# Down projection by seven block products in a fused two-block transformer kernel

## The reference, cut to what matters

```python
h2 = rms_norm_2(x, g_ffn)                                  # x: 512 x 1024
act = silu(h2 @ w_ffn_gate) * (h2 @ w_ffn_up)              # 512 x 2816
x = x + act @ w_ffn_down                                   # 2816 x 1024
return rms_norm_2(x, g_final)
```

## Time and profile before

| | us |
|---|---|
| median of 3 runs (1060.65 to 1061.04) | 1060.84 |
| the profiled execution, its span (the profile gives no other time of it) | 1059.3 |
| TensorE busy | 1049.7 (99%) |
| VectorE, ScalarE, GpSimd busy | 509.0 (48%), 448.8 (42%), 400.2 (38%) |
| HBM read and written | 92.80 MB and 2.12 MB |

### The profile page before, as it was taken

The page is one execution under the profiler, slowest core; times in us unless marked ns, Lnnn a source line. Parts: engine busy times, 40 slices in busy tenths (PEclk is TensorE's granted clock), DMA queues, the critical chain, the costliest instruction groups (busy, mean ns, idle before and its releaser), DMA issues.

```text
span 1059.3 us, 14455 instructions
## 1 busy us (share of the span) xinstructions
PE 1049.7 (99%) x5545; PEld 844.1 (80%) x5545; DVE 509.0 (48%) x1061; ACT 448.8 (42%) x788; POOL 400.2 (38%) x300
## 2 busy tenths in 40 slices
PE   9999999999999999999999999999999999999997
PEld 8877897767678876888777888888888888888886
DVE  6766788875752316998587344230000000032444
ACT  6444457676653425233465414342221221233533
POOL 3455520001025333446000255434435354465772
PEclk9999999999999999999999999999999999999999
DMA  9541141201032331332221232223232323323221
GB/s 298 184 120 51 34 119 41 75 17 44 28 120 80 72 117 43 101 99 80 80 80 41 80 104 95 91 77 110 80 118 79 114 84 104 114 80 100 82 97 80
DMA packets 84724, 95.72 MB, mean 90 GB/s; under 512 B 8121, under 2 KB 70930, under 8 KB 84666
## 3 DMA queue, kind: packets, MB, share of 16 engines
q1 hardware_dynamic: 83706, 92.46, 28.0%
q0 software_dynamic: 560, 2.12, 0.6%
q10 hardware_dynamic: 400, 0.35, 0.1%
HBM read 92.80 MB, written 2.12 MB: 90 GB/s over the span
## 4 chain that ended last, share of the span: by engine, by line
PE 94%; DVE 4%; ACT 1%; issue 1%; POOL 0%; DVEq 0%; ACTq 0%; POOLq 0%
PE bank L1882 56%; PE bank L2194 23%; PE bank L1940 4%; PE bank L1971 3%; PE bank L2012 3%; PE bank L1988 1%; DVE L L1478 1%; PE bank L2169 1%; PE bank L1833 1%; PE bank L2098 1%; PE bank L2045 1%; DVE L L1524 1%; DVE pool L1483 0%; PE bank L2001 0%; PE bank L1964 0%
## 5 line engine op out<-in xcount | busy, mean ns | idle before, releaser
L1042 POOL TENSOR_TENSOR w_lo<-raw,w_hi 128x512 fp32r<-128x512 f32 (+1 forms) x190 | 267.2, 1436 | 415.7 <-ACT w_hi L1104 403.0
L1882 PE MATMUL bank<-h_hi,w_hi 128*128 128x512 f32 (+1 forms) x560 | 224.0, 400 | 0.3 <-ACT h_hi L1315 0.2
L1882 PE MATMUL bank<-h_hi,w_lo 128*128 128x512 f32 (+1 forms) x560 | 218.6, 390 | 0.0
L1882 PE MATMUL bank<-h_lo,w_hi 128*128 128x512 f32 (+1 forms) x560 | 217.8, 390 | 0.0
L1082 POOL TENSOR_TENSOR w_lo<-raw,w_hi 128x512 fp32r<-128x512 f32 x88 | 110.7, 1290 | 133.5 <-ACT w_hi L1353 67.1
L1104 ACT ACTIVATE w_hi<-raw 128x512 fp32r<-128x512 f32 (+3 forms) x94 | 111.2, 1213 | 116.1 <-PE bank L1882 113.8
L1882 PE MATMUL bank<-w_hi,h_hi 128*128 128x512 f32 (+2 forms) x397 | 145.3, 366 | 0.0
L1882 PE MATMUL bank<-w_lo,h_hi 128*128 128x512 f32 (+2 forms) x397 | 144.5, 364 | 0.0
L1882 PE MATMUL bank<-w_hi,h_lo 128*128 128x512 f32 (+2 forms) x397 | 144.5, 364 | 0.0
L2194 PE MATMUL bank<-h_hi,w_hi 128*128 128x512 f32 x352 | 137.1, 389 | 0.0
L2194 PE MATMUL bank<-h_hi,w_lo 128*128 128x512 f32 x352 | 137.0, 389 | 0.0
(11 more groups left out here) (213 smaller groups left out, 1260.3 us busy)
## 6 DMA issues: line engine op xcount, KB each, us to landing
raw<-in_w_in SPq DMA_DIRECT2D x29, 1024.0 KB, 5.3
raw<-in_w_ffn_gate SPq DMA_DIRECT2D x11, 1024.0 KB, 5.4
raw<-in_w_ffn_up SPq DMA_DIRECT2D x11, 1024.0 KB, 5.4
raw<-in_w_out SPq DMA_DIRECT2D x8, 1024.0 KB, 5.0
raw<-in_w_ffn_down SPq DMA_DIRECT2D x8, 1024.0 KB, 5.1
raw<-in_w_in SPq DMA_DIRECT2D x8, 512.0 KB, 4.6
pool<-in_cmp_w SPq DMA_DIRECT2D x4, 1024.0 KB, 9.1
raw<-in_w_ffn_down SPq DMA_DIRECT2D x4, 768.0 KB, 4.3
```

The costliest lines, as they stand in the source:

```text
L1042: nc.gpsimd.tensor_tensor(w_lo[:, u.n % 2, cols], raw[:, u.n % 2, cols], w_hi[:, u.n % 2, cols].bitcast(F32), ALU.subtract).then_inc(lo_do ...
L1882: ins = mm(bank[t.bank][0:t.m, 0:u.width if u.token else T], stationary, moving, start=first and n == 0, stop=last and n == len(products) ...
```

## The change

With A the activations (rows: tokens, 0 to 255 and 256 to 511; columns: even and odd feature tiles) and B the weights (rows: even and odd tiles; columns: the two halves), the eight block products of A times B are replaced by seven with sums of blocks (Winograd's form of Strassen's scheme):

- on the activations: s1 and s2, the left factors of p5 and p6 (s1 from the blocks `s1` and `a22` of the buffer, s2 from s1 and `a11`), and s3 = a22 - s2 and s4 = a12 - s2, the left factors of p7 and p3;
- on the weights: t1 to t4, four sums of 128x512 per pair of weight tiles.

Each product has 11 weight tiles in units of 4, 4 and 3, and two token tiles (256 tokens). The order is p1, p6, p7, p5, p4, p3, p2. p3 and p2 go on accumulating in the banks of p5 and p1. p1 is copied out by ScalarE (kind "lead"); p6 and p7 are added by VectorE in two instructions each ("second", "third"); p5, p4, p3 and p2 end rows ("residual"). Rows 2 and 3 are finished before rows 0 and 1.

The sums of the activations s1 and s2 and all weight sums are made by VectorE in the feed-forward steps; the weight sums are stored in HBM by SyncE and loaded back as units. The temporaries s3 and s4 are made by VectorE unit by unit during the down projection. In all units but the first the low part of the first 512 columns is GpSimd's, the rest VectorE's, and ScalarE's high part is made in two instructions.

The diff, cut to its core:

```diff
+    def product_units(name, left_, right, banks, kind, tiles, more=False):
+        tiles = [Tile(0, P, kind, idx) for idx in tiles]
+        for f, n in ((0, 4), (4, 4), (8, 3)):
+            u = Unit(name, [(right(f, n), 0, 512)], n, 512, tiles, k0=f, first=f == 0, last=f == 8, act=True, token=True)
...
+    FIRST_ROWS, LATER_ROWS = (0, 1), (2, 3)
+    down_u = (product_units("p1", "a11", lambda f, n: down_block(0, 0, f, n), (0, 1), "lead", FIRST_ROWS)
+              + product_units("p6", "s2", lambda f, n: down_sum(1, f, n), (2, 3), "second", FIRST_ROWS)
+              + product_units("p7", "s3", lambda f, n: down_sum(2, f, n), (4, 5), "third", FIRST_ROWS)
+              + product_units("p5", "s1", lambda f, n: down_sum(0, f, n), (6, 7), "residual", [(1, i) for i in LATER_ROWS])
+              + product_units("p4", "a22", lambda f, n: down_sum(3, f, n), (4, 5), "residual", [(0, i) for i in LATER_ROWS])
+              + product_units("p3", "s4", lambda f, n: down_block(1, 1, f, n), (6, 7), "residual", [(1, i) for i in FIRST_ROWS],
+                              more=True)
+              + product_units("p2", "a12", lambda f, n: down_block(1, 0, f, n), (0, 1), "residual", [(0, i) for i in FIRST_ROWS],
+                              more=True))
+    LAST_ORDER = LATER_ROWS + FIRST_ROWS
+    POOL_PART = 1
...
-    project(down_u, RING4, 4)
+    for u in down_u:
+        for j, t in enumerate(u.tiles):
...
+            if j == 0 and next_of[u.n] is not None:
+                emit("split", u=next_of[u.n], of=u)
...
+            emit("matmuls", u=u, t=t, j=j, ks=range(u.nk), end=True, part=part, fresh=None)
+            if u.last and t.kind == "residual":
+                evacuated(t)
...
         def _(sp):
             def load(u):
                 if u.n >= 2:
-                    wait_free(sp, [(order[u.n - 2].lo_by, order[u.n - 2].lo_end)])
+                    wait_free(sp, order[u.n - 2].lo_all)
...
+            def load_blocks(f):
+                sp.dma_start(zs[:, 0:2, :], wdown.rearrange("(r p) n -> p r n", p=P)[:, bass.ds(f * 2, 2), :]).then_inc(blocks_in, 16)
+            def store_sums(f):
+                sp.wait_ge(sums_made, f * 1 + 1)
+                sp.dma_start(sums_dram[:, bass.ds(f * 2048, 2048)], zs[:, 2:4, :].rearrange("p a n -> p (a n)"))\
+                  .then_inc(sums_stored, 16)
+            ffn_loads(0)
+            ffn_loads(1)
+            sp.wait_ge(tile_done, ffn_at["tile"] + 1)
+            load_blocks(0)
+            with sp.Fori(2, FFN_STEPS) as f:
+                ffn_loads(f)
+                store_sums(f - 2)
+                load_blocks(f - 1)
+            store_sums(FFN_STEPS - 2)
+            load_blocks(FFN_STEPS - 1)
             sp.dma_start(gfin, a["g_final_2"].to_broadcast([P, D])).then_inc(gfin_in, 16)
             for u in down_u:
+                if u is down_u[3]:
+                    store_sums(FFN_STEPS - 1)
+                if u.summed:
+                    sp.wait_ge(sums_stored, 16 * (u.k0 + u.nk))
                 load(u)
...
         # ScalarE, at "split"
+                    if e["u"].shared:
+                        split_hi(e["u"], slice(0, POOL_PART * PIECE))
+                        split_hi(e["u"], slice(POOL_PART * PIECE, e["u"].nk * PIECE))
+                        split_act_hi(e["u"])
...
         # VectorE, at "split"
+                if kind == "split" and e["u"].shared:
+                    ahead_ = e["u"].act0 + 1
+                    if ahead_ < len(down_u) and down_u[ahead_] in temps:
+                        make_temp(down_u[ahead_])
+                    split_shared(e["u"])
+                    split_act_lo(e["u"])
...
+            def split_shared(u):
+                ve.wait_ge(hi_done, u.hi_end)
+                cols = slice(POOL_PART * PIECE, u.nk * PIECE)
+                v.tensor_tensor(w_lo[:, u.n % 2, cols], raw[:, u.n % 2, cols], w_hi[:, u.n % 2, cols].bitcast(F32),
+                                ALU.subtract).then_inc(lo_dve, 1)
...
+                if kind == "second":
+                    chain(v.tensor_tensor(L[:, idx, :], src[:, :], L[:, idx, :], ALU.add))
+                    v.tensor_tensor(x, x, L[:, idx, :], ALU.add).then_inc(second_done, 1)
+                if kind == "third":
+                    chain(v.tensor_tensor(L[:, idx, :], src[:, :], L[:, idx, :], ALU.add))
+                    x = xres[:, 2 + idx, :].rearrange("p (c n) -> p c n", n=512)
+                    v.tensor_tensor(x, x, spread(L[:, idx, 0:1], [0, 2], [1, 512]), ALU.add).then_inc(third_done, 1)
...
+                    def left_sums(f):
+                        v.tensor_tensor(s1, s1, left_pair(f, LEFT["a22"]), ALU.add).then_inc(left_made, 1)
+                        v.tensor_tensor(left_pair(f, LEFT["s2"]), s1, left_pair(f, LEFT["a11"]), ALU.subtract)\
+                            .then_inc(left_made, 1)
+                    def block_sums(f, first=False):
+                        ve.wait_ge(blocks_in, f * 16 + 16)
...
+                        v.tensor_tensor(t1, block_in[:, 0, 1, :], block_in[:, 0, 0, :], ALU.subtract).then_inc(sum_step, 1)
+                        v.tensor_tensor(t3, block_in[:, 1, 1, :], block_in[:, 0, 1, :], ALU.subtract)
+                        v.tensor_tensor(t2, block_in[:, 1, 1, :], t1, ALU.subtract).then_inc(sum_step, 1)
+                        v.tensor_tensor(t4, block_in[:, 1, 0, :], t2, ALU.subtract).then_inc(sums_made, 1)
...
+                    gated_step(0)
+                    block_sums(0, first=True)
+                    gated_step(1)
+                    with ve.Fori(2, FFN_STEPS - 1) as f:
+                        block_sums(f - 1)
+                        gated_step(f)
+                    block_sums(FFN_STEPS - 2)
+                    gated(FFN_STEPS - 1, 0, left_pair(FFN_STEPS - 1, 0, 512))
                     split_act_lo(down_u[0])
-                    gated(FFN_STEPS - 1, 1, act[:, NFF - 1, :])
+                    gated(FFN_STEPS - 1, 1, left_pair(FFN_STEPS - 1, 512, 512))
+                    left_sums(FFN_STEPS - 1)
+                    block_sums(FFN_STEPS - 1)
```

More of the change, by code:

```diff
@@ L693, in build @@
         u.used = ("tile_done", ffn_at["tile"] + 2 * j + 2)
-    turn[RING4] = 0
-    project(down_u, RING4, 4)
-    flush()
+    ffn_end = count["tile_done"]
+    for u in down_u:
+        for j, t in enumerate(u.tiles):
+            if u.first:
+                t.bank = u.banks[j]
+                t.waits = left[t.bank]
+            if j == 0 and next_of[u.n] is not None:
+                emit("split", u=next_of[u.n], of=u)
+            unit_end = j == len(u.tiles) - 1
+            t.done = upto("tile_done") if u.last else None
+            part = upto("part_done") if unit_end and not u.last else None
+            if unit_end:
+                u.used = ("part_done", part) if part else ("tile_done", t.done)
+            emit("matmuls", u=u, t=t, j=j, ks=range(u.nk), end=True, part=part, fresh=None)
+            if u.last and t.kind == "residual":
+                evacuated(t)
+            elif u.last:
+                t.nth = upto(t.kind + "_done")
+                left[t.bank] = [(t.kind + "_done", t.nth)]
+                emit("evacuate", t=t)
     units_before_ffn = order[:ffn_u[0].n]
@@ L1011, in _, with ffn_loads @@
             n0 = ffn_u[0].n
[L1012 removed]
+            def ffn_loads(f):
                 for j, w in enumerate((wg, wu)):
@@ L1216, in row @@
                 else:
-                    if half == 0 and i == 0:
+                    if (half, i) == ((1, LAST_ORDER[0]) if nth == 3 else (0, 0)):
                         act_fn(st[:, ST_RS + NT:ST_RS + NT + 1], eps, ACT.Sqrt)
@@ L1685, in last_rows @@
             def last_rows(half, i, res):
-                if half and i == NT - 1:
+                final, p = half == 0, LAST_ORDER.index(i)
+                if final and p == NT - 1:
                     ve.wait_ge(squares, squares_at(3, half, i))
@@ L1689, in last_rows @@
                                     st[:, ST_BASE + i:ST_BASE + i + 1], ALU.mult, ALU.add).then_inc(base_done, 1)
-                if half and i == 0:
-                    ve.wait_ge(squares, squares_at(3, 0, NT - 1))
-                    v.tensor_scalar(st[:, ST_BASE:ST_BASE + NT], st[:, ST_SS:ST_SS + NT], 1.0 / D, EPS, ALU.mult, ALU.add)\
-                        .then_inc(base_done, 1)
-                if half:
-                    gained(half, i, res)
-                if half and i != NT - 2:
+                if final and p in (0, 2):
+                    ve.wait_ge(squares, squares_at(3, 1, i + 1))
+                    v.tensor_scalar(st[:, ST_BASE + i:ST_BASE + i + 2], st[:, ST_SS + i:ST_SS + i + 2], 1.0 / D, EPS,
+                                    ALU.mult, ALU.add).then_inc(base_done, 1)
+                gained(half, i, res)
+                if final and p != NT - 2:
                     last_row(i)
@@ L1881, in matmuls @@
                         wait_free(pe, [(h_hi_at, h_lo_at)[p][fresh, u.k0 + k]])
```

(4 more changed lines are left out.)

187 lines of the change are left out of this document (131 added, 56 removed).

## The result

| | before | after |
|---|---|---|
| median, us (range, runs) | 1060.86 (1060.65 to 1061.04, 4) | 1083.32 (1081.06 to 1084.01, 4) |
| span of the profiled execution, us | 1059.3 | 1081.8 |
| ratio after / before | | 1.0208, 95% interval 1.0194 to 1.0223 |

The change made the kernel 2.1% slower, 22.5 us. Forecast were +13.5 us and a range up to 1081. The direction was right, the size was not, and the measured time lies outside the range.

A forecast was written before the change was run, and what follows sets the result against it. The down projection was taken to be bound by TensorE alone. Terms -15.0 + 7.2 + 12.0 + 9.8 - 0.5 = +13.5 on 1060.8 gave 1074.3 us, range 1065 to 1081.

The forecast's parts named there:

- Removed matmuls: Down projection: seven block products instead of eight, 462 matmuls instead of 528, 15.0 us less.
- First units: Start of each product after the first: TensorE waits 1.2 us for a_lo, six times, 7.2 us.
- Second units: Second units of products: evacuations and row work delay their splits, longest wait 4.8 us after p4, sum 12.0 us.
- Hand-over: Feed-forward to down projection: late first load and VectorE's queue make the second down unit start 9.8 us late.
- Taking turns: Hand-over: VectorE and GpSimd alternate, one whole instruction each; without it and with the load in time, 1.6 us.
- The reading as both running slower: Hand-over: VectorE and GpSimd slow side by side, by 27% and 40%; second unit near 944, sum 4.4 us smaller.
- Tail: End of kernel: one row instead of three before the last tile, so its second half is evacuated earlier, -0.5 us.
- rival 3: Down projection: clock also falls in two new gaps, one or two units at double pitch, 1077 to 1084; chance 0.13.

The follow-up runs named there:

- e4: The changed kernel with the activations' high and low parts and temporaries made one unit further ahead; 1068.19 us.
- e5: The changed kernel with evacuations and row work of a product's two tiles moved behind the split of the next product's second unit; 1070.97 us.
- e2: The changed kernel with the first down unit's load issued on SyncE ahead of the store of step 9's sums; 1077.51 us.
- e9: The changed kernel with first down load issued first, last block sums behind the second unit's splits, their store before the sixth unit's load; 1072.86 us.
- e1: The changed kernel with float32 matmuls on constants queued on TensorE before five of its long waits; 1075.76 us.
- e7: The changed kernel with first down load first, last block sums late, activations one unit further ahead, row work behind the next product's second-unit split; 1058.88 us.
- e10: The changed kernel with half of the low parts on GpSimd instead of a quarter; 1088.22 us.
- e11: e8 with two float32 fill matmuls before the first unit of p2; 1053.95 us.
- e8: e7 with the last sums' store before the sixth unit's load and row work's two tiles split behind the successor's second and third units; 1056.16 us.

## Why the prediction was right and wrong

- **Removed matmuls, -15.0**: right, same pitch.
- **First units, 7.2**: right (7.6). e4 took a_lo out of the chain and the waits went.
- **Second units, 12.0**: right in sum (12.1), and that near by luck: the longest was 5.7, not 4.8, and two others 0.4 shorter than forecast. That the evacuations queue behind the next first unit's splits, and that row work holds w_hi, both read from the earlier trace rows, is borne out by e5, which moved the two together and nothing else.
- **Hand-over, 9.8**: right (9.0). The load landed at 931.8 (932.7 forecast), the last block sum of step 9 ended at 919.7 (919.6), a_lo of u1 at 947.9 (948.5). e2 and e9 show that both the load and VectorE's queue are behind it; the load moved alone did not suffice (e2), the sums moved alone were not run.
- **Taking turns**: right; 5.57 for four a_lo (1.54 in e2 without GpSimd) and 2.29 for the one of u1 are waits for GpSimd pieces. The reading as both running slower, with 4.4 us less, is out: u1 started at 947.9, not near 944. A turn was shorter than forecast, 1.43 us by the starts at 935.46, 936.89, 938.32 and 939.74 against 1.6.
- **Tail**: -0.3 instead of -0.5.
- **The step that failed** is the one that left the clock out of the sum and made it rival 3, with chance 0.13. I took from the earlier trace rows that the clock stays up for 3.8 us of standstill and asked only of gaps that long. It fell after some 2 us of the gap before u1, and behind two gaps of 2.0 us as well; so one fall in the tail, after a long dense run, is no bound for how short a gap may be. It was four falls and 7.2 us by the traces (e1 gave back 7.6 by the medians), of the 9.0 by which the forecast was short; the other terms were short by some 1.8 in sum, nearly all of it small delays that the forecast put at nothing (the 1.6 of the table).
- **Rival 3** named the right mechanism, and its time, 1077 to 1084, holds the measured one, but by luck in the number: it counted one or two falls at up to 5.4 us each, a whole unit at half clock, and there were four at 1.5 to 2.1. Its upper end should have been the end of the range.
- **What stays open** is why the gaps of 2.0 us before the second units of p4 and p2 were enough, while eight of 1.1 to 1.5 us, the 1.95 us before u0 and the 2.8 us of e7 and e10 were not.
- The Trainium skill's rule (TensorE: Matmul & The Clock Gate, Part 1), that the clock is at half after an idle stretch until activity has been sustained, agrees with the windows behind the gaps of 4.7 and 5.7 us. Its rule on the shared port (SBUF — State Buffer, Who interferes with whom) agrees with 2.29 against 1.22, one GpSimd piece more; the turns of 1.43 are shorter than the two instructions one after the other (0.42 and 1.26 by the rows), so in part they overlapped.

## What to carry to other kernels

Seven products in place of eight took an eighth of the matmuls off, and since each product has half the tokens, they also halved the time under which a unit's preparation must fit (48 matmuls to 24). With such a change, add up one unit's chain over the engines' queues in order, at both kinds of edges, and compare it with the new cover before counting the saving. In a queue in order, a store that waits for late data holds every load written behind it. Where a change opens gaps on TensorE, price each at its length, read the granted clock behind it rather than trust a length, and count some 2 us more for each one behind which it is down (7.2 over four here).

## What was not expected of the hardware

The clock fell behind gaps of 2.0 us (window 1064.30: 0.61, with DMA share 0.00), after TensorE had taken up work again, and some 8 matmuls then ran 0.43 apart; behind 2.8 us in e7 it did not fall. Two float32 matmuls before one unit (1.88 us) were enough to keep it at 1.00 in e11, and the runs' spread fell from 2.5 us (e8) to 0.5 us. Giving GpSimd a second piece of 1.3 us a unit cost 4.9 us in all: 16 of the 20 a_lo behind u0's took about 1.1 us longer by a turn (2 of 20 in after), and before first units, where a_lo ends the chain, this is the longer wait.
